# Three kinds of small TensorE work moved into the middle of the attention slots, and PSUM units given by hand

## The chip, the cores and the metric

The kernel runs on one core of one Trainium2 chip. The metric is the device time of one execution in microseconds. Before the change it is 1381.16 us, the median of 3 runs (1380.94 to 1382.31). The core has five engines, each with its own instruction stream in program order: TensorE (PE, matrix products, with weight loads shown apart as PEld), VectorE (DVE), ScalarE (ACT), GpSimd (POOL) and SyncE (SP, which only starts transfers here). They meet at semaphores.

## The reference

Two transformer blocks on 256 tokens of 1024 channels, in fp32. The change touches the first block. It makes one wide projection `h @ w_in` and feeds three branches:

```
(c_glu, c_gate, d_q, d_k, d_v, d_gate, x_q, x_gate, merge) = jnp.split(
    h @ w_in[l], IN_SPLITS, axis=-1)
y_conv = conformer_conv_branch(c_glu, c_gate, ...)   # 31-tap causal convolution per channel, layer norm
y_diff = differential_attention_branch(d_q, d_k, d_v, d_gate, ...)   # 8 heads, two softmaxes each
y_mem  = memory_cross_attention_branch(x_q, x_gate, mem_h, w_mem_kv, ...)  # 4 heads over 256 memory rows
y = g[:, :, 0] * y_conv + g[:, :, 1] * y_diff + g[:, :, 2] * y_mem
x = x + y @ w_out[l]
```

In the differential branch q and k are normed per head (a sum of squares over 64 channels), each head has `a = p[:, :, 0] - lam * p[:, :, 1]` with `p` a causal softmax, and the output `a @ v` is normed over 128 channels. The memory branch norms q and k over 256 channels and has plain softmaxes. The second block (stick-breaking attention, an RG-LRU, and a lookup of 16 experts for each of 8 heads) follows.

## The kernel before, in words

All projections are cut into **slots** of 512 output columns. A slot is two **pieces** of 256 columns. For a piece the queue of SP loads 1 MB of weights into `w_raw`; ACT rounds them into `w_hi` (L667, `hi(p)`), DVE writes the rest into `w_lo` (L1117, `lo(p)`); and PE makes 48 matrix products of 256 columns (L368: high by high, high by low, low by high). `w_hi` and `w_lo` have three buffers, so `hi(p)` waits until PE has finished piece p-3, and the two engines split the pieces of slot n+1 while PE works on slot n. On ACT and DVE the function `ahead(s)` does this, one piece after the other, and can run a list of functions `between` the two. `project(s)` on PE has such a list too; in the attention slots before the change it is empty.

The order of every engine is written out by hand. The list `attention` has 18 slots: n = 0 to 5 are q0, k0, v0, q1, k1, v1, 6 and 7 are xq0 and xq1, 8 and 9 xk0 and xk1, 10 and 11 xv0 and xv1, 12 to 17 the merge gates m0 to m5. Around each slot stand the steps of the attention, skewed against each other so that each finds its input ready:

- `head_sums`: ones times squares (L401, L407), for the q or k of the slot before. Its square comes from ACT (L737), and after it come a Ln and an Exp on ACT (L744, L749) and a scaling on DVE (L1221). `diff_norm_sums` (L417) is the same for the attended heads, half dn0 (heads 0 to 3) and dn1; its square is L788 on ACT, which stands there behind the exponentials (L768) of the head of that slot. ACT does the squares of dn0 at the end of n = 10, and PE sums them at n = 11.
- `diff_scores(h)` at n = h+3 (L429), then on DVE the softmax of that head (L1243 to L1268) with the exponentials on ACT (L768) in its middle; `diff_turn(h)` at n = h+4 transposes the probabilities (L439), ACT copies them from PSUM (L776), and `diff_values(h)` at n = h+5 multiplies with v (L448, L449). `cross_scores`, `cross_turn`, `cross_values` (L459, L470, L481) do the same for the memory heads at n = h+11, h+12 and h+13.
- `turn_input("mem")` transposes the normed memory (L389) into the second input pair, ahead of slot v0 (n = 2). Slots xk0 and later use it.
- Between its pieces DVE also does three taps of the convolution each (L1132). POOL does five of the eight channel tiles of the convolution alone (L1762, L1766). `conv_mean` on PE (L492), after the slots dg0 and dg1 which follow the attention slots, waits for all eight tiles.

PSUM is three **units** of two banks and two single banks, each a ring: `take` gives the next one in turn, and a user waits until the prior holder's readers have marked it free. Slots, sums and scores all take units in the order in which they stand on PE.

## Time and profile before

| what | value |
|---|---|
| device time, median of 3 | 1381.16 us |
| the profiled execution, own time | 1380.68 us |
| its span in the trace | 1378.9 us |
| PE busy, share of span | 84% |
| DVE, ACT, POOL busy | 70%, 41%, 41% |
| mean granted PE clock | 0.975 of full |

The span begins at 0 and all times below count from there. The 18 attention slots run from about 72 to 349 us, slots dg0 and dg1 to 371.8 us, the rest of the first block to about 529 us. From about 700 us on the expert lookup runs, with the transfer engines busy 96% of the time. A timeline row gives start, length, engine, line, operation, names and shape, and in brackets the idle time of the engine ahead of it with what ended it. Matrix products overlap, so 96 of them that start 0.12 us apart show 0.28 us each; an fp32 product is two records, one of the rounded type is one.

### The profile page before, as it was taken

What the parts mean: (1) busy time and instruction counts of PE and PEld (TensorE: products, weight loads), DVE (VectorE), ACT (ScalarE), POOL (GpSimd) and SP (SyncE); (2) the same over time, 40 slices, a digit from 0 to 9 for tenths busy, and PEclk for the clock granted to TensorE, in tenths of its full rate; (3) what the DMA queues carried; (4) which work ended last, traced back from release to release, by engine and by line L of the source; (5) the groups of instructions that cost most, each with busy time, mean ns of one, the idle gap of its engine ahead of it and who ended that gap; (6) DMA issues with size and microseconds to landing.
All of it is one profiled execution on the core that took longest, in us unless ns stands there. A gap on an engine that the chain in (4) does not pass through costs nothing.

```text
span 1378.9 us, 16624 instructions
## 1 busy us (share of the span) xinstructions
PE 1163.5 (84%) x6104; PEld 819.6 (59%) x6104; DVE 972.0 (70%) x1937; ACT 569.0 (41%) x1022; POOL 561.9 (41%) x576
## 2 busy tenths in 40 slices
PE   5999898999999998976898877777877777777787
PEld 5999788899999998975895322222322222222222
DVE  4488888894567655656577777777777777777554
ACT  5376656664345334885342322222222222222221
POOL 0099999999600000000023434444444444444431
PEclk9999999999999999998999999999999999999999
DMA  6644343354536644420458999999999999999995
GB/s 222 198 139 143 102 123 123 122 163 153 174 123 218 210 153 152 147 92 31 153 181 335 424 426 424 424 425 423 425 424 425 424 424 419 422 413 404 425 425 226
DMA packets 137331, 374.43 MB, mean 272 GB/s; under 512 B 6816, under 2 KB 103072, under 8 KB 104352
## 3 DMA queue, kind: packets, MB, share of 16 engines
q0 software_dynamic: 36864, 268.45, 46.8%
q1 hardware_dynamic: 98048, 99.62, 22.3%
q10 hardware_dynamic: 2336, 5.29, 1.1%
q8 instruction: 48, 0.79, 0.2%
q14 instruction: 35, 0.29, 0.1%
HBM read 372.29 MB, written 1.05 MB: 271 GB/s over the span
## 4 chain that ended last, share of the span: by engine, by line
PE 38%; DMA 34%; DVE 16%; ACT 6%; issue 5%; ACTq 0%; POOL 0%; POOLq 0%; DVEq 0%
PE unit L368 29%; DMA big<-in_experts,big 16%; DMA row<-in_experts,big 7%; DMA w_raw<-in_experts,big 6%; PE unit L585 6%; DMA conv_in<-in_experts,big 5%; DVE w_lo L1117 3%; DVE conv_acc L1132 3%; DVE work L1464 2%; ACT probs L899 1%; ACT probs L768 1%; DVE big L1221 1%; DVE probs L1264 1%; DMA w_raw<-in_w_in 1%; DVE probs L1268 1%
## 5 line engine op out<-in xcount | busy, mean ns | idle before, releaser
L368 PE MATMUL unit<-in_hi,w_hi 128*128 128x256 f32 x1216 | 351.8, 289 | 8.7 <-DVE probs L1336 4.8
L368 PE MATMUL unit<-in_lo,w_hi 128*128 128x256 f32 x1216 | 347.3, 286 | 0.0
L368 PE MATMUL unit<-in_hi,w_lo 128*128 128x256 f32 x1216 | 347.2, 286 | 0.0
L1117 DVE TENSOR_TENSOR w_lo<-w_raw,w_hi 128x2048 fp32r<-128x2048 f32 x94 | 219.0, 2332 | 122.7 <-ACT w_hi L667 122.7
L899 ACT ACTIVATE probs<-ident,big 128x128 f32<-128x128 f32 x256 | 102.8, 401 | 462.9 <-DVE big L1476 462.9
L585 PE MATMUL unit<-big,probs 128*128 128x512 f32 x452 | 224.0, 621 | 63.9 <-ACT probs L899 63.8
L368 PEld LDWEIGHTS unit<-in_hi,w_hi 128*128 128x128 f32 x1216 | 237.2, 195 | 11.2 <-issue 5.9
L368 PEld LDWEIGHTS unit<-in_lo,w_hi 128*128 128x128 f32 x1216 | 237.0, 195 | 0.9 <-issue 0.7
L1774 POOL DMA_INDIRECT row<-in_experts,big x58 | 63.5, 1095 | 426.9 <-DVE big L1457 343.4
L368 PEld LDWEIGHTS unit<-in_hi,w_lo 128*128 128x128 f32 x1216 | 236.7, 195 | 0.0
L667 ACT CAST w_hi<-w_raw 128x2048 fp32r<-128x2048 f32 x94 | 177.0, 1899 | 128.9 <-PE unit L368 84.7
L585 PEld LDWEIGHTS unit<-big,probs 128*128 128x128 f32 x452 | 79.5, 191 | 204.8 <-ACT probs L899 144.4
L1774 POOL DMA_INDIRECT big<-in_experts,big x113 | 120.0, 1062 | 168.2 <-PE unit L585 151.9
L1464 DVE CUSTOM_DVE_ANT_0 work<-big 128x1024 f32<-128x1024 f32 x113 | 138.0, 1222 | 65.7 <-DMA big<-in_experts,big 65.7
L585 PE MATMUL unit<-row,probs 128*128 128x512 f32 x232 | 116.9, 634 | 33.0 <-ACT probs L899 32.8
L1766 POOL TENSOR_TENSOR conv_acc<-conv_acc,big 128x256 f32<-128x256 f32 x150 | 139.5, 930 | 12.5
L1762 POOL TENSOR_SCALAR big<-conv_in,vec 128x256 f32<-128x256 f32 x150 | 141.5, 944 | 2.9
L585 PE MATMUL unit<-w_raw,probs 128*128 128x512 f32 x224 | 109.6, 619 | 27.4 <-ACT probs L899 27.3
L585 PEld LDWEIGHTS unit<-row,probs 128*128 128x128 f32 x232 | 41.5, 195 | 106.0 <-ACT probs L899 74.2
L585 PEld LDWEIGHTS unit<-w_raw,probs 128*128 128x128 f32 x224 | 39.4, 191 | 95.2 <-ACT probs L899 65.7
L1464 DVE CUSTOM_DVE_ANT_0 work<-big,row 128x1024 f32<-128x1024 f32 x58 | 70.7, 1221 | 31.2 <-DMA row<-in_experts,big 31.2
L1774 POOL DMA_INDIRECT w_raw<-in_experts,big x56 | 60.1, 1073 | 77.2 <-PE unit L585 68.7
(246 smaller groups left out, 1699.0 us busy)
## 6 DMA issues: line engine op xcount, KB each, us to landing
w_raw<-in_w_in SPq DMA_DIRECT2D x58, 1024.0 KB, 5.2
w_raw<-in_w_mem_kv SPq DMA_DIRECT2D x8, 1024.0 KB, 5.3
w_raw<-in_w_out SPq DMA_DIRECT2D x8, 1024.0 KB, 5.2
w_raw<-in_w_query SPq DMA_DIRECT2D x8, 1024.0 KB, 5.4
w_raw<-in_w_diff_proj SPq DMA_DIRECT2D x4, 1024.0 KB, 5.6
w_raw<-in_w_x_proj SPq DMA_DIRECT2D x4, 1024.0 KB, 5.1
w_raw<-in_w_conv_proj SPq DMA_DIRECT2D x4, 1024.0 KB, 5.2
big<-in_x ACTq DMA_DIRECT2D x2, 1024.0 KB, 7.5
```

What stands on the lines that cost most here:

```text
L368: m = e.matmul(unit[:, to:to + 256], fixed, moving, start=start, stop=stop)
L585: m = e.matmul(unit[:, half * 512:(half + 1) * 512], diag_places[g % 12], UV.ap(g)[:, D + half * 512:D + (half + 1) * 512], start=n == 0, ...
L667: e.copy(w_split[p % 3][0][:, :, :], w_raw[p % 2][:, :, :]).then_inc(*mark("hi", p))
L768: a = e.activation(p[:, m, c], p[:, m, c], ACT.Exp, bias=few[:, i + m:i + m + 1], accum_out=few[:, 4 + i + m:5 + i + m])
L899: e.activation(diag_places[g % 12], ident[:, :], ACT.Copy, scale=here).then_inc(*mark("diag", g))
L1117: e.tensor_tensor(lo_part[:, :, :], w_raw[p % 2][:, :, :], hi_part[:, :, :].bitcast(F32), ALU.subtract).then_inc(*mark("lo", p))
L1132: i = e.scalar_tensor_tensor(out=dst, in0=src, scalar=tap, in1=dst, op0=ALU.mult, op1=ALU.add)
L1221: i = e.scalar_tensor_tensor(out=part, in0=part, scalar=gain[:, j:j + 1], in1=work.ap(name)[:, 0:n].rearrange("p (g t) -> p g t", t=T), op ...
L1464: e.tensor_tensor_reduce(out=work.ap(("dot", g))[:, 0:D], in0=h3[:, t, :], in1=UV.ap(g)[:, 0:D], scale=1.0, scalar=0.0, op0=ALU.mult, op1= ...
L1762: e.tensor_scalar(product, src, tap, 1.0, ALU.mult, ALU.mult).then_inc(*mark("pool_product", (t, k)))
L1766: e.tensor_tensor(dst, dst, product, ALU.add).then_inc(*mark("pool_tap", None, *done))
L1774: e.indirect_dma_start(out=UV.ap(g), out_offset=None, in_=experts, in_offset=bass.IndirectOffsetOnAxis(ap=expert[t][:, n:n + 1], axis=0)). ...
```

## The change

On PE the sums of squares, the transposes of the probabilities and the turn of the memory are no longer done around a slot; they are handed to `project` as a list that runs between its two pieces. ACT (Ln, Exp, copy of the transposed probabilities, rounding of the memory) and DVE (scaling, the rest of the memory) move along into the middle of their `ahead`. The transposes of head h move from behind slot h+4 to the middle of slot h+5 (cross heads: from behind h+12 to the middle of h+13), the turn of the memory from ahead of slot 2 to the middle of slot 3, and the sums from behind slot n to its middle. `take` accepts a unit number: slots alternate between units 0 and 1, sums take the one of the two that the running slot does not have, scores always take unit 2. The values of head 7 stand in the common place, behind slot 12.

```
     def take(self, use, place=None):
-        i = self.n % len(self.buffers)
-        self.n += 1
+        i = self.n % len(self.buffers) if place is None else place
+        self.n = i + 1
...
 # PE
             for n, s in enumerate(attention):
-                if s.name == "v0":
-                    turn_input("mem", mem_tm,
-                               lambda half: (("scaled", "mem", half, 0), ("scaled", "mem", half, 1)))
-                project(s)
-                if s.name == "m0":
-                    diff_values(DIFF_HEADS - 1)
+                midway, other = [], 1 - n % 2
                 if pending in HEAD_NORMS:
-                    head_sums(pending)
+                    midway.append(partial(head_sums, pending, other))
                 elif pending:
-                    diff_norm_sums(int(pending[2:]))
+                    midway.append(partial(diff_norm_sums, int(pending[2:]), other))
+                if s.name == "q1":
+                    midway.append(partial(turn_input, "mem", mem_tm, lambda half: (
+                        ("scaled", "mem", half, 0), ("scaled", "mem", half, 1)), (other, 2)))
+                if 0 <= n - 5 < DIFF_HEADS:
+                    midway.append(partial(diff_turn, n - 5))
+                if 0 <= n - 13 < X_HEADS:
+                    midway.append(partial(cross_turn, n - 13))
+                project(s, midway, n % 2)
                 pending = s.name if s.name in HEAD_NORMS else {10: "dn0", 12: "dn1"}.get(n)
-                if 0 <= n - 5 < DIFF_HEADS - 1:
+                if 0 <= n - 5 < DIFF_HEADS:
                     diff_values(n - 5)
-                if 0 <= n - 4 < DIFF_HEADS:
-                    diff_turn(n - 4)
...
-            project(slot["dg0"])
+            project(slot["dg0"], place=0)
...
 # ACT
-                if name == "v0":
-                    turn_input("mem", "mem_norm_g")
-                ahead(s)
+                midway = []
+                if pending in HEAD_NORMS:
+                    midway.append(partial(head_root, pending))
+                elif pending:
+                    midway.append(partial(inverse_root, pending, 4 * T, P))
+                if name == "q1":
+                    midway.append(partial(turn_input, "mem", "mem_norm_g"))
+                if 0 <= n - 5 < DIFF_HEADS:
+                    midway.append(partial(diff_turned, n - 5))
+                if 0 <= n - 13 < X_HEADS:
+                    midway.append(partial(cross_turned, n - 13))
+                ahead(s, between=midway)
...
 # DVE
-                ahead(s)
+                midway = []
+                if pending in HEAD_NORMS:
+                    midway.append(partial(head_scale, pending))
+                elif pending:
+                    midway.append(partial(diff_norm_scale, pending))
+                if s.name == "q1":
+                    midway.append(partial(turn_input, "mem", "mem_norm_g"))
+                ahead(s, between=midway)
```

PE at the end of slot 11 (xv1) before. L417 is the sum of squares of dn0 (its squares lie in `work0`), L448 and L449 the values of head 6, L439 the transposes of head 7, L459 the scores of memory head 0:

```order
L368 MATMUL unit2<-w1_hi,in1_hi 128x256
L368 MATMUL unit2<-w1_hi,in1_lo 128x256
L368 MATMUL unit2<-w1_lo,in1_hi 128x256
L417 MATMUL unit0<-work0,ones 128x512 x2
L448 MATMUL bank1<-probs_t0,big2 128x256
L449 MATMUL bank1<-probs_t0,big2 128x128
L439 MATMUL bank0<-ident,probs1 128x128 x3
L459 MATMUL unit1<-big5,big4 128x256 x4
L368 MATMUL unit2<-in0_hi,w2_hi 128x256
```

PE in the middle of slot 11 now, between its piece in `w0` and its piece in `w1` (lines are one higher in the changed file). L418 is the sum of squares of dn0, L440 the transposes of head 6:

```order
L369 MATMUL unit1<-w0_hi,in1_hi 128x256
L369 MATMUL unit1<-w0_hi,in1_lo 128x256
L369 MATMUL unit1<-w0_lo,in1_hi 128x256
L418 MATMUL unit0<-work0,ones 128x512 x2
L440 MATMUL bank0<-ident,probs0 128x128 x3
L369 MATMUL unit1<-w1_hi,in1_hi 128x256
```

The sum of dn0 has moved ahead of the second piece of the same slot, 48 products earlier than before; head 7's transposes are no longer there and stand in the middle of slot 12.

ACT at the same place before, from the exponentials of head 7 (L768) over the squares of dn0 (L788) to the Ln and Exp of dn0 (L744, L749) and the copy of head 7's transposed probabilities (L776):

```order
L768 ACTIVATE probs1,col<-probs1,col 128x256 x2
L768 ACTIVATE probs1,col<-probs1,col 128x128 x2
L788 ACTIVATE work0<-big0 128x1024
L667 CAST w2_hi<-w_raw0 128x2048
L667 CAST w0_hi<-w_raw1 128x2048
L759 COPY big6<-unit2 128x2x512
L744 ACT_TABLE_LOAD
L744 ACTIVATE work0<-unit0,col 128x1024
L749 ACT_TABLE_LOAD
L749 ACTIVATE work0<-work0 128x1024
L782 COPY big0<-bank1 128x256
L776 COPY probs_t1<-bank0 128x384
```

And now, the same span of ACT:

```order
L768 ACTIVATE probs1,col<-probs1,col 128x256 x2
L768 ACTIVATE probs1,col<-probs1,col 128x128 x2
L788 ACTIVATE work0<-big0 128x1024
L667 CAST w2_hi<-w_raw0 128x2048
L744 ACT_TABLE_LOAD
L744 ACTIVATE work0<-unit0,col 128x1024
L749 ACT_TABLE_LOAD
L749 ACTIVATE work0<-work0 128x1024
L776 COPY probs_t0<-bank0 128x384
L667 CAST w0_hi<-w_raw1 128x2048
L759 COPY big6<-unit1 128x2x512
L782 COPY big0<-bank1 128x256
```

Ln, Exp and the copy of the probabilities have moved between the two castings; the squares of dn0 keep their place behind the exponentials of head 7.

## Rows read from the trace of the kernel before

**Rows 1.** Windows: length, busy PE, PEld, DVE, ACT, POOL, then clock, DMA share, GB/s.

```profile
200.00:250.00 50.00, 42.99 (x316) 40.46 (x315) 44.69 (x55) 33.77 (x50) 47.75 (x54) 0.97 0.35 110
300.00:350.00 50.00, 50.00 (x395) 49.06 (x394) 28.98 (x24) 22.19 (x22) 45.84 (x49) 1.00 0.48 153
```

**Rows 2.** Waits from 150 to 263 us: total, times, longest.

```profile
DVE col L1257 <- ACT probs L768: 11.6, 6, 1.9
PE bank L439 <- DVE probs L1268: 9.5, 5, 4.0
PE unit L368 <- DVE w_lo L1117: 4.0, 5, 0.8
PE unit L417 <- ACT work L788: 2.1, 1, 2.1
```

**Rows 3.** Timeline of DVE, one slot's round.

```profile
222.65 2.28 DVE L1117 TENSOR_TENSOR w_lo<-w_raw,w_hi 128x2048 fp32r<-128x2048 f32 x1
...
231.45 2.11 DVE L1221 SCALAR_TENSOR_TENSOR big<-big,vec,work 128x512 f32<-128x512 f32 x2
...
237.84 0.18 DVE L1257 RECIPROCAL col<-col 128x4 f32<-128x4 f32 x1 [1.93 <-ACT probs L768]
...
241.12 2.28 DVE L1117 TENSOR_TENSOR w_lo<-w_raw,w_hi 128x2048 fp32r<-128x2048 f32 x1
```

**Rows 4.** Timeline of ACT, the readers of slots dg0 and dg1.

```profile
360.49 1.02 ACT L818 ACTIVATE work<-unit 128x1024 f32<-128x1024 f32 x1 [3.80 <-PE unit L368]
...
372.01 1.02 ACT L818 ACTIVATE work<-unit 128x1024 f32<-128x1024 f32 x1 [3.80 <-PE unit L368]
```

**Rows 5.** The page's group of the castings on ACT: busy and mean ns of one.

```profile
L667 ACT CAST w_hi<-w_raw 128x2048 fp32r<-128x2048 f32 x94 | 177.0, 1899 | 128.9 <-PE unit L368 84.7
```

**Rows 6.** Timeline of ACT, slots 10 and 11.

```profile
242.33 1.28 ACT L744 ACT_TABLE_LOAD   x1
243.62 0.69 ACT L744 ACTIVATE work<-unit,col 128x512 f32<-128x512 f32 x1
...
256.20 1.04 ACT L788 ACTIVATE work<-big 128x1024 f32<-128x1024 f32 x1
```

**Rows 7.** Timeline of PE, from slot 11 to the start of slot 12.

```profile
243.45 0.39 PE L368 MATMUL unit<-w_hi,in_hi 128*128 128x256 f32 x1 [0.79 <-DVE w_lo L1117]
...
257.29 3.09 PE L417 MATMUL unit<-work,ones 128*128 128x512 f32 x4 [2.06 <-ACT work L788]
260.17 1.06 PE L448 MATMUL bank<-probs_t,big 128*128 128x256 f32 x2
...
261.78 1.89 PE L459 MATMUL unit<-big 128*128 128x256 f32 x8
263.32 0.47 PE L368 MATMUL unit<-in_hi,w_hi 128*128 128x256 f32 x1
```

**Rows 8.** Timeline of DVE, its idle times ahead of the first softmax.

```profile
97.54 1.37 DVE L1221 SCALAR_TENSOR_TENSOR big<-big,col,work 128x1024 f32<-128x1024 f32 x1 [0.76 <-ACT work L749]
...
112.90 1.33 DVE L1221 SCALAR_TENSOR_TENSOR big<-big,vec,work 128x1024 f32<-128x1024 f32 x1 [1.62 <-ACT work L749]
```

**Rows 9.** Windows of PE: length, busy, granted clock, DMA share, GB/s.

```profile
169.20:172.70 3.50, 3.46 (x16) 0.51 0.06 8
258.00:261.40 3.40, 3.40 (x7) 0.50 0.02 5
529.20:534.50 5.30, 5.30 (x25) 0.50 0.01 3
```

**Rows 10.** Timeline of POOL, its last products.

```profile
351.94 2.51 POOL L1762 TENSOR_SCALAR big<-conv_in,vec 128x256 f32<-128x256 f32 x1
...
355.37 0.48 POOL L1762 TENSOR_SCALAR big<-conv_in,vec 128x256 f32<-128x256 f32 x1
...
368.02 0.74 POOL L1766 TENSOR_TENSOR conv_acc<-conv_acc,big 128x256 f32<-128x256 f32 x1
```

**Rows 11.** Timeline of PE, conv_mean.

```profile
371.81 3.61 PE L492 MATMUL unit<-conv_acc,ones 128*128 128x256 f32 x16
```

More of the change, by code:

```diff
@@ L1 @@
 from contextlib import ExitStack
+from functools import partial
 import concourse.bass as bass
@@ L91, in __init__, with take @@
         self.place, self.prior, self.holder, self.n = {}, {}, [None] * len(buffers), 0
-    def take(self, use):
-        i = self.n % len(self.buffers)
-        self.n += 1
+    def take(self, use, place=None):
+        i = self.n % len(self.buffers) if place is None else place
+        self.n = i + 1
         self.place[use], self.prior[use], self.holder[i] = i, self.holder[i], use
@@ L342, in pe, with project @@
             W = Reached(at)
-            def project(s, between=()):
-                unit = units.take(s.name)
+            def project(s, between=(), place=None):
+                unit = units.take(s.name, place)
                 in_hi, in_lo = pairs.ap(s.pair)
@@ L376, in project, with turn_input @@
                             f()
-            def turn_input(pair, src, scaled):
+            def turn_input(pair, src, scaled, places=(None, None)):
                 for half in range(2):
                     name = f"{pair} turn{half}"
-                    unit = units.take(name)
+                    unit = units.take(name, places[half])
                     for bank in range(2):
@@ L391, in turn_input, with head_sums @@
                         m.then_inc(*mark("turned", (pair, 2 * half + bank)))
-            def head_sums(name):
-                sq, unit = work.ap(name), units.take(name + " sums")
+            def head_sums(name, place=None):
+                sq, unit = work.ap(name), units.take(name + " sums", place)
                 for wait in W(("sq", name), units.free(name + " sums"), ("const", None)):
@@ L409, in head_sums, with diff_norm_sums @@
                 m.then_inc(*mark("sums", name))
-            def diff_norm_sums(i):
+            def diff_norm_sums(i, place):
                 name = f"dn{i}"
-                sq, unit = work.ap(name), units.take(name + " sums")
+                sq, unit = work.ap(name), units.take(name + " sums", place)
                 for wait in W(("sq", name), units.free(name + " sums")):
@@ L421, in diff_scores @@
             def diff_scores(h):
-                unit = units.take(f"d{h}")
+                unit = units.take(f"d{h}", 2)
                 for wait in W(("normed", f"q{h // 4}"), ("normed", f"k{h // 4}"),
@@ L452, in cross_scores @@
             def cross_scores(h):
-                unit = units.take(f"x{h}")
+                unit = units.take(f"x{h}", 2)
                 for wait in W(("normed", f"xq{h // 2}"), ("normed", f"xk{h // 2}"),
@@ L613, in pe @@
                     cross_values(n - 13)
-                if 0 <= n - 12 < X_HEADS:
-                    cross_turn(n - 12)
                 if 0 <= n - 11 < X_HEADS:
                     cross_scores(n - 11)
-            project(slot["dg0"])
+            project(slot["dg0"], place=0)
             project(slot["dg1"])
@@ L951, in act @@
                         *mark("merge", i, ("unit free", name)))
-                if pending in HEAD_NORMS:
-                    head_root(pending)
-                elif pending:
-                    inverse_root(pending, 4 * T, P)
                 pending = name if name in HEAD_NORMS else {10: "dn0", 12: "dn1"}.get(n)
@@ L958, in act @@
                     diff_attended(n - 5)
-                if 0 <= n - 4 < DIFF_HEADS:
-                    diff_turned(n - 4)
                 if 0 <= n - 3 < DIFF_HEADS:
@@ L966, in act @@
                     cross_attended(n - 13)
-                if 0 <= n - 12 < X_HEADS:
-                    cross_turned(n - 12)
                 if 0 <= n - 11 < X_HEADS:
@@ L1535, in dve @@
             for n, s in enumerate(attention):
-                if s.name == "v0":
-                    turn_input("mem", "mem_norm_g")
-                ahead(s)
+                midway = []
[6 more added lines that the diff above has]
+                ahead(s, between=midway)
                 if n == 0:
@@ L1541, in dve @@
                     scale_tokens("mem", mem_tm, mem_tm)
-                if pending in HEAD_NORMS:
-                    head_scale(pending)
-                elif pending:
-                    diff_norm_scale(pending)
                 pending = s.name if s.name in HEAD_NORMS else {10: "dn0", 12: "dn1"}.get(n)
```

## The prediction

> **What bounds the kernel now.** I read the busy shares by windows first, then the waits of the attention slots, then one slot as a timeline. The windows show two regimes. From 200 to 250 us PE is busy 43 of 50 us and DVE 44.7; from 300 to 350 us PE is busy all 50 and DVE 29 [rows 1]. So PE waits for something only in the slots with a differential softmax. The waits say for what: 9.5 us ahead of the transposes L439 until DVE has the probabilities, 4.0 us ahead of the next slot, 2.1 us ahead of the sum of squares dn0 (L417) until ACT has the squares [rows 2]. The first two make 13.5 us, which a better order on PE seems to be able to take back.
>
> The timeline of DVE says that it can't. Its round from one first `w_lo` to the next is 241.12 - 222.65 = 18.5 us, and all its idle time in it is the 1.93 us that it waits for the exponentials of its own softmax [rows 3]; that pair is also its whole wait in the list, 11.6 us in 6 times [rows 2]. It does not wait for PE there. PE's own work in such a slot is 11.5 us for the 96 products (the readers of two bare slots start at 360.49 and 372.01, 11.52 apart [rows 4]) and some 4 us for the small steps. Up to the end of the softmax of head 7 the pace is DVE's, whatever order PE has; after that it is PE's own.
>
> **The change part by part.**
>
> *Transposes and scores.* No instruction is added or removed on PE, DVE or ACT; all terms are about places. The transposes of head h go half a slot or more behind the end of its softmax, so the wait of L439 goes. What is late next is the values: they need the copy that ACT makes of the transposes, and it stands now behind the exponentials of the next head, a casting, and Ln and Exp. With the exponentials done at 237.8 [rows 3], a casting of 1.9 [rows 5], two table loads with two functions of twice 1.29 + 0.7 = 4.0 [rows 6] and about 0.5 for the copy, the values could start at 244.2, and with some 1.5 us of values and scores (both estimates) slot 11 starts about 245.7, where it starts now at 243.45 [rows 7]. So PE still stands still some 3 us in each slot, in another place. All of it lies beside DVE, whose next softmax needs those scores at 241.12 + (231.45 - 222.65) + 2.1 = 252.0 [rows 3], 6 us later. Gain 0, cost 0.
>
> *Scaling on DVE.* It stands now one `w_lo` and three taps after the softmax, (231.45 - 222.65)/2 = 4.4 us behind 241.12, at 245.5 [rows 3], and needs Ln and Exp, which are done at 237.8 + 1.9 + 4.0 = 243.7 for the 512 wide ones and about 0.9 later for the 1024 wide ones. That holds with 0.9 us to spare at least. Cost 0. If the cover went, each microsecond would count in each of the six slots, since DVE sets the pace.
>
> Here a rule speaks against the change. The trace shows a load of 1.28 us and the Ln 1.29 us behind the load's start [rows 6]. The Trainium skill (ScalarE: Activation LUTs, What ACT_TABLE_LOAD costs) says that a switch of sets costs a drain beside its load, about 2.66 us in all. By that rule two switches would take 2.7 us more than my sum, the scaling would wait up to 1.9 us per slot, and the time would be some 8 us longer still. By the row nothing happens, and I go by the row.
>
> *Start.* Ahead of the first softmax DVE waits 0.76 and 1.62 us for Ln and Exp [rows 8]. Sums that are taken half a slot earlier can shorten this. The bounds are 0 and 2.4 us; as the scaling also moves forward, it keeps part of the wait. I take 1.0 us gained; call it G.
>
> *The sum of squares dn0.* This is the term that decides. Its squares (L788) stand on ACT behind the exponentials of head 7, which are the end of DVE's part in the softmax of slot 10. They are ready at 256.20 + 1.04 = 257.24 [rows 6], or 257.24 - G, by DVE's pace. Now PE has finished all of slot 11 by then and waits 2.06 us. After the change it has done only the first piece, waits (from about 251 until 256, by the slot start above), and has the second piece still to do: 11.52/2 = 5.76 us [rows 4] that used to lie under DVE's pace come behind it. From there on PE waits for nothing [rows 1] and all of it counts. Cost 5.76 - G = 4.8 us.
>
> *The clock.* PE's granted clock is 0.50, the lower level, 1.2 GHz, in 258.0 to 261.4, behind the wait of 2.06 us, and in another place it stays at 0.50 for 5.3 us [rows 9]. In the first, half of 3.4 us is lost, 1.7 us; the sum took 3.09 there [rows 7]. After the change PE idles some 5 us ahead of dn0 and would start at about 256.2. If the clock comes back at 261.4 as now, 5.2 us run at half, 2.6 lost, 0.9 more than before. Bounds: 0 more, and 2.65 (half of the 5.3 us of the other place on top). I take 0.9.
>
> *Turn of the memory, units, cross heads.* The turn is the same 16 + 8 + 8 instructions one slot later, needed first in slot xk0; the cross heads' transposes sit in PE's own stream with the same length; with fixed units a slot waits for the copy of the slot two before. None has a wait in PE's stretch after 263 now [rows 1], each has half a slot of room. Bounds -0.5 and +1; I take 0.
>
> *conv_mean.* POOL's last product ends at 368.76 [rows 10], and conv_mean starts at 371.81 right behind dg1 [rows 11]. A later PE only widens that. Everything behind it hangs on it, and shifts as a whole.
>
> Sum: 4.8 + 0.9 = 5.7 us later, so 1380.7 + 5.7 = 1386.4 us against the profiled execution; that one was 0.5 below the median of the runs, so I say 1386.6.
>
> **The rivals.**
>
> *A. Not slower: the waits go and POOL becomes the bound.* If DVE's pace were not binding and PE took back its 13.5 us, it would reach conv_mean at 358 and wait for POOL until 368.8. But DVE runs ahead with PE: the `w_lo` of the next slot then falls under POOL's last products, and a POOL product beside a `w_lo` takes 2.51 where it takes 0.48 otherwise [rows 10], 2 us. That ends POOL at about 370.8, a gain of 1.0, or of 3.0 at best without this. PE would have idled 10 us and would start conv_mean at the low clock, 1.7 to 2.65 lost: 1380.7 - 3.0 + 1.7 to 1380.7 - 1.0 + 2.65, so 1379.4 to 1382.4. It decides from the point at which PE reaches conv_mean before 368.8. Against it: DVE's round has no idle time that PE could give back.
>
> *B. The early gain is larger and pays for dn0.* G at its upper bound 2.4 and no further loss of clock: 5.76 - 2.4 = 3.4, so 1384.1, 1384.3 against the median. G above 3 would end inside no change. For it: both idle times of rows 8 wait for just the operations that move.
>
> *C. The scaling on DVE waits in every slot.* It starts once Ln and Exp are 0.9 us later than assumed; up to 1 us beyond that in six slots is 1 to 6 us on top: 1388 to 1393. For it: the margin is thin, and a contention with other work could use it up. Against: the row of the load, which shows nothing beside the load itself [rows 6]. The drain of the Trainium skill's page (ScalarE: Activation LUTs, What ACT_TABLE_LOAD costs) would be this case.
>
> *D. Faster by clearly more than the bound*, if the sum dn0 finds its squares ready. ACT would have to do them 6 us earlier than DVE lets it. I see nothing for it.
>
> **How the numbers follow.** Forecast (shift 4.0 to 7.5 with the clock's bounds) 0.66; B 0.10; A 0.10; C 0.10; D and unknown gains 0.04. What a measurement of this kernel can tell from no change is 0.2%, 2.8 us: faster is under 1378.4, slower over 1384.0. Faster takes D and a little of A, 0.05; the same takes the rest of A and a third of B, 0.12; slower the other cases, 0.83. The range 1382.4 to 1389.4 holds the forecast with its bounds, B, the top of A and the bottom of C.
>
> **What would show it.** Right: the transposes have no wait; the values (L449 in the changed file) wait some 3 us per slot for ACT's copy; DVE's round stays at 18.5 us; L418 of dn0 waits 4 to 7 us for ACT's squares at about 256 us and the clock behind it is 0.5; conv_mean starts at about 377.5, with no wait, and each later stage is later by the same amount. Wrong: a shorter round of DVE, a wait of conv_mean for POOL (A), idle time ahead of L1222 in slots 4 to 9 (C), or a sum dn0 without a wait (D).

## The result, and the profile after

The changed kernel takes 1388.53 us (median of 13 runs, 1384.30 to 1389.59) against 1381.16 us (13 runs, 1379.34 to 1382.31): 7.4 us slower by the medians. The ratio is 1.0048 with a 95% interval of 1.0039 to 1.0057; that is the ratio of the means, 1387.75 and 1381.08 us, 6.7 us apart. The 13 times of the changed kernel lie in two groups, five from 1384.30 to 1386.99 us and eight from 1388.46 to 1389.59, and the median is in the longer one. The profiled execution, 1385.57 us, is of the shorter group, 4.9 us over the profiled one of before.

| | before | after |
|---|---|---|
| profiled execution, own time | 1380.68 | 1385.57 us |
| span | 1378.9 | 1383.8 us |
| mean granted PE clock, profiled execution | 0.975 | 0.970 |
| PE busy, share of span | 84% | 84% |
| DVE, ACT, POOL busy | 70%, 41%, 41% | 70%, 41%, 40% |

The waits of PE and DVE from 150 to 263 us in the kernel after (total, times, longest), against [rows 2]:

```profile
DVE col L1258 <- ACT probs L768: 11.6, 6, 1.9
PE bank L449 <- ACT probs_t L776: 9.7, 4, 3.3
PE unit L418 <- ACT work L788: 5.6, 1, 5.6
PE unit L369 <- DVE w_lo L1118: 1.7, 1, 1.7
```

The transposes (L440) don't wait any more; the values (L449) do, 9.7 us where the transposes had 9.5. DVE's own wait is the same 11.6 us. And dn0 waits 5.6 us for its squares instead of 2.1.

The timeline of PE after, from the end of slot 10 to slot 12, and conv_mean, against [rows 7, 11]:

```profile
240.99 0.70 PE L449 MATMUL bank<-probs_t,big 128*128 128x256 f32 x2 [0.22 <-ACT probs_t L776]
...
242.70 0.39 PE L369 MATMUL unit<-w_hi,in_hi 128*128 128x256 f32 x1
...
254.28 3.78 PE L418 MATMUL unit<-work,ones 128*128 128x512 f32 x4 [5.56 <-ACT work L788]
257.85 0.85 PE L440 MATMUL bank<-ident,probs 128*128 128x128 f32 x3
258.35 0.56 PE L369 MATMUL unit<-w_hi,in_hi 128*128 128x256 f32 x1
...
266.82 0.47 PE L369 MATMUL unit<-in_hi,w_hi 128*128 128x256 f32 x1
...
375.62 3.61 PE L493 MATMUL unit<-conv_acc,ones 128*128 128x256 f32 x16
```

Slot 11 starts at 242.70 (243.45 before), its sum dn0 at 254.28 (257.29 before), but slot 12 at 266.82 (263.32 before): the second piece of slot 11 now stands behind the sum. conv_mean starts at 375.62 without an idle time (371.81 before).

The timeline of DVE after, two rounds:

```profile
216.37 0.18 DVE L1258 RECIPROCAL col<-col 128x4 f32<-128x4 f32 x1 [1.93 <-ACT probs L768]
...
234.87 0.18 DVE L1258 RECIPROCAL col<-col 128x4 f32<-128x4 f32 x1 [1.93 <-ACT probs L768]
...
253.31 0.18 DVE L1258 RECIPROCAL col<-col 128x4 f32<-128x4 f32 x1 [1.93 <-ACT probs L768]
```

The rounds are 18.50 and 18.44 us, those before 18.48 and 18.48. Before, the reciprocal of head 6 stood at 237.84 [rows 3] and that of head 7 here:

```profile
256.32 0.18 DVE L1257 RECIPROCAL col<-col 128x4 f32<-128x4 f32 x1 [1.93 <-ACT probs L768]
```

**A fixed point to count from.** The start of the span moves between executions. DVE's second write of `conv_in`, right ahead of the attention slots, is the same step in every kernel, at 68.62 us before and at 67.79 after, and at 67.40 to 68.82 over the 14 profiles. The timeline of DVE, before and then after:

```profile
68.62 1.22 DVE L1528 SCALAR_TENSOR_TENSOR conv_in<-work,unit 128x1024 f32<-128x1024 f32 x1 [2.54 <-ACT work L921]
```

```profile
67.79 1.22 DVE L1529 SCALAR_TENSOR_TENSOR conv_in<-work,unit 128x1024 f32<-128x1024 f32 x1 [2.54 <-ACT work L921]
```

The first three columns count from it: the reciprocal of head 7 on DVE, the start of slot 12 on PE, and conv_mean. "Round" is the mean of the seven rounds between the eight reciprocals, the last two columns are the time from conv_mean to the turn of the second block's input, and from there to the end of the span. All in us, from one profile each.

| kernel | head 7 | slot 12 | conv_mean | round | to turn | to end |
|---|---|---|---|---|---|---|
| before | 187.70 | 194.70 | 303.19 | 18.21 | 157.35 | 849.7 |
| after | 185.52 | 199.03 | 307.83 | 18.11 | 155.85 | 852.3 |
| after_again | 185.54 | 198.15 | 306.95 | 18.11 | 157.35 | 849.3 |
| after_again2 | 185.61 | 198.96 | 307.75 | 18.12 | 157.35 | 850.8 |
| before_dn0_mid | 187.09 | 199.97 | 308.47 | 18.26 | 157.35 | 850.2 |
| before_heads_mid | 185.51 | 191.39 | 302.99 | 18.05 | 159.10 | 849.8 |
| before_turns_mid | 187.14 | 193.07 | 302.72 | 18.27 | 157.61 | 852.5 |
| after_dn0_next | 185.47 | 191.10 | 303.69 | 18.07 | 159.03 | 850.0 |
| after_squares | 185.53 | 196.48 | 305.28 | 18.11 | 158.98 | 851.8 |
| heads_mid_pool4 | 186.38 | 192.24 | 302.23 | 18.22 | 158.96 | 853.0 |
| after_squares_pool4 | 185.45 | 196.92 | 306.31 | 18.14 | 159.03 | 849.8 |
| after_squares_pool4_taps | 175.92 | 186.77 | 298.08 | 16.83 | 159.14 | 849.1 |
| turns_first | 185.58 | 191.19 | 302.45 | 18.12 | 155.83 | 852.4 |
| tile_shared | 164.77 | 172.42 | 287.84 | 15.41 | 157.43 | 851.6 |

Read along the second row: head 7 comes 2.2 us earlier, slot 12 is 4.3 us later, conv_mean 4.6 us. Up to the turn 1.5 us are got back, by the clock (last section), and behind it 2.6 are lost, at least in part by the clock; with the 0.8 us by which the fixed point comes earlier that makes 4.9.

The row "before" is itself one profile. before_dn0_mid, whose order up to slot 10 is the old one, has head 7 at 187.09, 0.6 us earlier than the profile of before. So the early gain is 1.6 to 2.2 us.

### The profile page after: what moved, and what is told of

Read it like the earlier page. It is cut to its first block, busy times and chain, and to the rows that moved or that the text cites. A ratio compares the mean times of both kernels' runs of the same rounds, so it can differ in the third digit from the quotient of the medians.

```text
span 1383.8 us, 16623 instructions
## 1 busy us (share of the span) xinstructions
PE 1164.6 (84%) x6104; PEld 819.8 (59%) x6104; DVE 972.1 (70%) x1937; ACT 569.1 (41%) x1022; POOL 555.8 (40%) x576
## 4 chain that ended last, share of the span: by engine, by line
PE 38%; DMA 34%; DVE 18%; ACT 6%; issue 5%; ACTq 0%; POOL 0%; POOLq 0%; DVEq 0%
PE unit L369 27%; DMA big<-in_experts,big 16%; DMA row<-in_experts,big 7%; PE unit L586 6%; DMA w_raw<-in_experts,big 6%; DMA conv_in<-in_experts,big 5%; DVE w_lo L1118 4%; DVE conv_acc L1133 3%; DVE work L1465 2%; ACT probs L768 1%; ACT probs L899 1%; DVE probs L1265 1%; DMA w_raw<-in_w_in 1%; DVE big L1222 1%; DVE probs L1269 1%
## 5 line engine op out<-in xcount | busy, mean ns | idle before, releaser
L1768 POOL TENSOR_TENSOR conv_acc<-conv_acc,big 128x256 f32<-128x256 f32 x150 | 143.2, 954 | 12.5
L1764 POOL TENSOR_SCALAR big<-conv_in,vec 128x256 f32<-128x256 f32 x150 | 133.3, 889 | 2.9
```

The source lines that it names most:

```text
L1764: e.tensor_scalar(product, src, tap, 1.0, ALU.mult, ALU.mult).then_inc(*mark("pool_product", (t, k)))
L1768: e.tensor_tensor(dst, dst, product, ALU.add).then_inc(*mark("pool_tap", None, *done))
```

## Experiments

Times are medians; ratios are to the kernel before, run on the same chip, with the 95% interval.

**after_dn0_next: dn0 in the middle of slot 12.** On PE, ACT and DVE alike:

```
-                pending = s.name if s.name in HEAD_NORMS else {10: "dn0", 12: "dn1"}.get(n)
+                pending = s.name if s.name in HEAD_NORMS else {11: "dn0", 12: "dn1"}.get(n)
```

> The changed kernel with one difference: the sum of squares dn0, with its Ln, Exp and scaling, stands in the middle of slot 12 and no longer of slot 11 (dn1 stays in slot 13). Theory 'place of dn0': in the trace of the changed kernel slot 12 starts at 266.82 us because dn0 waits for its squares until 254.28 with half of slot 11 still to do. Without it slot 11 ends at about 254, and slot 12 waits for its w_lo, which is written at 258.8, so it starts at about 259; dn0 then costs 1.9 us as a sum without a wait, and conv_mean starts at 375.6 - 7.8 + 1.9 = 369.7 us instead of 375.62. The time is 5 to 6 us under the changed kernel and about 2 us under the kernel before: 1378 to 1381 us. Theory 'clock': the changed kernel loses its time to twice as much low clock in the slots (three stretches of 6.8 us against three of 3.4 us), which waits in every slot bring about; then the place of dn0 gives back 1 to 2 us only, 1386 to 1388 us.

Measured: 1383.23 us, ratio 1.0016 (1.0007 to 1.0025), 5.3 us under the changed kernel by the medians (4.4 by the ratios, 0.0032 of 1381). Against the kernel before it is slower, not 2 us faster as expected. Slot 12 starts at 258.50 us, as worked out. PE's timeline:

```profile
258.50 0.39 PE L369 MATMUL unit<-in_hi,w_hi 128*128 128x256 f32 x1
...
264.35 1.88 PE L418 MATMUL unit<-work,ones 128*128 128x512 f32 x4
...
274.20 0.70 PE L449 MATMUL bank<-probs_t,big 128*128 128x256 f32 x2 [1.89 <-ACT probs_t L776]
```

The place of dn0 is the larger part of the loss, and the theory of the clock, which expected 1386 to 1388 us, falls. But of 7.9 us at slot 12 only 4.1 are left at conv_mean: the sum costs 1.9 there, and the values of head 7 wait 1.89 us for a copy that now stands behind Ln and Exp of dn0, a wait that I had not counted. Against the kernel before it is 0.5 us late at conv_mean, and 1.7 more go behind it (last section).

**before_dn0_mid: the one part alone, in the kernel before.** Its three places follow the same pattern:

```
-                project(s)
+                mid = pending == "dn0"
+                project(s, [step] if mid else ())     # step: the sum of the name in pending
...
+                if step and not mid:
+                    step()
```

> The kernel before, in which the sum of squares dn0 alone (with Ln, Exp and scaling) moves into the middle of slot 11. Theory 'place of dn0': the half slot of 5.76 us that lay ahead of the wait comes behind it, nothing is gained earlier, and the low clock takes up to 2 us more: conv_mean at 377.5 to 379.5 us, 1387 to 1389 us. Theory 'clock' (the loss comes from waits in all slots): dn0 alone costs 0 to 2 us, 1381 to 1383 us.

Measured: 1386.66 us, ratio 1.0049 (1.0036 to 1.0062). PE's timeline:

```profile
256.02 3.78 PE L418 MATMUL unit<-work,ones 128*128 128x512 f32 x4 [6.30 <-ACT work L790]
...
267.94 0.47 PE L369 MATMUL unit<-in_hi,w_hi 128*128 128x256 f32 x1
```

This one move gives the ratio of the whole change, with a wait of 6.30 us. From head 7 to slot 12 it is 267.94 - 255.06 = 12.9 us instead of 263.32 - 256.32 = 7.0, 5.9 more (255.06 is the reciprocal of head 7 in this run). conv_mean is 5.3 us later by the table. The expectation was 377.5 to 379.5 us for conv_mean and 1387 to 1389 for the time; they are 376.44 and 1386.66, just under both. Its six times lie in two groups too: four from 1385.60 to 1387.15 us and two at 1390.15 and 1390.59.

**before_heads_mid: only the sums of q, k, xq, xk.** As above with `mid = pending in HEAD_NORMS`.

> The kernel before, in which only the sums of squares of q, k, xq and xk (with Ln, Exp and scaling) move into the middle of the next slot; dn0, dn1, the transposes and the memory's turn stay. Theory 'early gain': all of the 3.0 us by which the exponentials of head 7 came earlier in the changed kernel (253.31 against 256.32 us) come from these sums. The sum dn0 starts at about 254.3, conv_mean at 368.8 to 369.3 us (the last product on POOL ends at 368.8), and the time is 2.5 to 3 us under the kernel before: about 1378.5 us. Rival: the gain comes from the transposes, whose wait went; then this kernel stays at 1381 us.

Measured: 1381.63 us, ratio 1.0003 (0.9995 to 1.0012). The time was expected 2.5 to 3 us lower and is unchanged. In the table head 7 comes 2.2 us earlier (1.6 against before_dn0_mid), exactly as in the changed kernel: these sums are all of the early gain. Slot 12 is 3.3 us earlier. But PE and POOL at conv_mean show where it ends:

```profile
370.70 5.38 PE L493 MATMUL unit<-conv_acc,ones 128*128 128x256 f32 x16 [2.95 <-issue]
```

```profile
369.31 0.48 POOL L1766 TENSOR_SCALAR big<-conv_in,vec 128x256 f32<-128x256 f32 x1
369.88 0.72 POOL L1770 TENSOR_TENSOR conv_acc<-conv_acc,big 128x256 f32<-128x256 f32 x1
```

conv_mean starts 0.1 us behind POOL's last product and has 2.95 us idle ahead of it, and behind that the clock is low (5.38 us for 3.61). The early gain came as expected, but POOL's end does not stay at 368.8: its last product ends at 370.6 us, and counted from the fixed point it is 2.8 us later (302.89 against 300.14).

**before_turns_mid: only the transposes.**

```
-                project(s)
+                project(s, [lambda: diff_turn(n - 5) if 0 <= n - 5 < DIFF_HEADS else None,
+                            lambda: cross_turn(n - 13) if 0 <= n - 13 < X_HEADS else None])
...
-                if 0 <= n - 4 < DIFF_HEADS:
-                    diff_turn(n - 4)
```

> The kernel before, in which only the transposes of the probabilities (differential and memory heads, with the copies on ACT) move half a slot back. Theory of the prediction: PE's wait moves from the transposes to the values, DVE's round stays at 18.5 us, and the time is 1381 us within 1 us. Rival: the transposes are what gave the 3.0 us, or a part above the 2.3 us of the start (0.7 us): 1378 to 1380.5 us. Rival 'clock': the waits that are then shorter and more frequent cost low clock, 1383 to 1385 us.

Measured: 1380.69 us, ratio 0.9998 (0.9989 to 1.0006). PE's waits from 150 to 263 us:

```profile
PE unit L368 <- DVE w_lo L1111: 7.6, 5, 1.8
PE bank L448 <- ACT probs_t L773: 4.9, 4, 3.0
```

13.5 us of waits were [rows 2], 12.5 are these: they moved and DVE's round stayed, 18.27. In the time there is no gain and no cost. On the way slot 12 is 1.6 us earlier than in the profile of before, with 0.6 of it there at head 7 already, as in before_dn0_mid, and no low stretch behind dn0; POOL then ends at 370.29 us, 0.1 us ahead of conv_mean.

**after_squares: ACT's squares ahead of the exponentials of head 7.**

```
+                if n == 10:
+                    diff_norm_squares(0)
                 if 0 <= n - 3 < DIFF_HEADS:
                     diff_exps(n - 3)
-                if n == 10:
-                    diff_norm_squares(0)
```

> The changed kernel with two steps of ACT exchanged at the end of slot 10: the squares of dn0 stand ahead of the exponentials of head 7 and no longer behind them. ACT is idle for 7.49 us there in the trace of the changed kernel, and the squares need only heads 0 to 3. Theory 'the wait of dn0 is one for ACT's order': the squares are ready at about 245 us, L418 has no wait, and the next thing that is late is the values of head 6, whose copy stands behind Ln and Exp of dn0: exponentials done at 253.2, casting 1.9, Ln and Exp with their loads 4.7, copy 0.46, so 260.3; with 2.2 us of values and scores slot 12 starts at 262.5 us instead of 266.82, conv_mean at 371.3 instead of 375.62, and the time is 4 to 5 us under the changed kernel: 1381.5 to 1384 us. Theory 'the cost is the pace of DVE and the clock, not this wait': 1387 to 1389 us.

Measured: 1383.37 us, ratio 1.0022 (1.0012 to 1.0031), 5.2 us under the changed kernel by the medians, 3.6 by the ratios. PE's timeline:

```profile
249.25 1.88 PE L418 MATMUL unit<-work,ones 128*128 128x512 f32 x4
...
261.02 1.07 PE L449 MATMUL bank<-probs_t,big 128*128 128x256 f32 x2 [3.81 <-ACT probs_t L776]
...
264.99 0.47 PE L369 MATMUL unit<-in_hi,w_hi 128*128 128x256 f32 x1
```

Its sum dn0 has no wait. As expected the values are what is late next; they come 0.7 us later than worked out, and the clock is low behind their wait (1.07 us for 0.59), so that slot 12 and conv_mean gain 2.6 us by the table, not 4.3. The time lies in the expected range, but this path gives only half of the 5.2 us; the rest of the difference of the medians it does not explain.

**heads_mid_pool4 and after_squares_pool4: POOL with four tiles.**

```
-POOL_TILES = (3, 4, 5, 6, 7)
+POOL_TILES = (4, 5, 6, 7)
...
-                ahead(s, between=midway)
+                ahead(s, between=midway, convolve=3 if n < 11 else 4)
```

In heads_mid_pool4, which is the kernel before with the sums of the heads moved, the list is `[step] if mid else ()` in place of `midway`.

> The kernel before with the sums of squares of q, k, xq and xk in the middle (as in before_heads_mid), and with one of the five convolution tiles of POOL given to DVE (POOL does tiles 4 to 7; DVE four taps per gap instead of three from slot 11 on). In before_heads_mid slot 12 started at 259.10 us, 4.2 us earlier than in the kernel before, but conv_mean started at 370.70, with 2.95 us idle ahead, right behind POOL's last product at 370.60. Theory 'POOL ends the gain': without that tile conv_mean starts at 259.1 + 108.5 = 367.6 us with no idle time ahead, and the time is 3 us lower than before_heads_mid: 1378 to 1379 us. Rival 'the early slots' gain is given back elsewhere' (DVE with 31 more taps, or the clock): 1381 to 1383 us.

> As after_squares, with POOL doing tiles 4 to 7 alone (DVE four taps per gap from slot 11 on). Theory 'POOL is not the bound here': POOL's last product ended at 364.2 us in the changed kernel and PE came to conv_mean at 375.6, and with the squares first at 371.3, so a shorter POOL gives nothing: the same time as after_squares within 1 us, unless POOL's products beside DVE's work slow DVE, where a shorter round of DVE would give 1 to 3 us.

Measured: heads_mid_pool4 1380.83 us, ratio 0.9999 (0.9989 to 1.0009); after_squares_pool4 1384.60 us, 1.0031 (1.0020 to 1.0041). The second is 1.2 us over after_squares where at most 1 us was expected, with overlapping intervals: relieving POOL gives nothing there. The profile of the first is its longest of 12 executions (1384.81 us; they go from 1378.15), so its stages are weak evidence. In it the idle time ahead of conv_mean is gone, but conv_mean comes only 0.8 us earlier than in before_heads_mid, not 3: from slot 12 it takes 110.0 us and not 108.5, with waits for DVE that has the tile now (the transposes of a memory head wait 0.76 us for its softmax). It does not decide between POOL and "given back elsewhere"; both are there.

**after_squares_pool4_taps: fewer taps where DVE sets the pace.**

```
-                ahead(s, between=midway, convolve=3 if n < 11 else 4)
+                ahead(s, between=midway, convolve=3 if n < 3 else 2 if n < 11 else 4)
...
-            convolve_some(len(taps))
...
-                ahead(slot[f"dg{i}"])
+                ahead(slot[f"dg{i}"], convolve=4)
+                if i == 1:
+                    convolve_some(len(taps))
```

> As after_squares_pool4, with the taps of the convolution on DVE moved out of the slots that DVE paces: two per gap instead of three in slots 3 to 10, four in slots 11 to 17 and in dg0 and dg1. Theory 'DVE's round paces slots 3 to 10': each round has two taps fewer, 1.4 us at 2.10 us for three, so the round falls from 18.5 to 17.1 us, the exponentials of head 7 end 8 x 1.4 = 11 us earlier, at about 242 us, conv_mean starts at about 360 us, and the time is 10 us under after_squares_pool4: 1370 to 1374 us. Rival 'PE's wait for ACT's copy sets the round as well': the round stays over 18 us and less than 4 us is gained, 1378 to 1382 us.

Measured: 1378.30 us, ratio 0.9979 (0.9970 to 0.9988). The round falls by 1.3 us, as expected, and head 7 comes 9.5 us earlier. The time, expected at 1370 to 1374 us, misses that by 4.3: slot 12 is 10.2 us earlier, conv_mean 8.2, with 0.99 us of waiting for the last taps on DVE (PE's timeline):

```profile
366.84 3.72 PE L493 MATMUL unit<-conv_acc,ones 128*128 128x256 f32 x16 [0.99 <-DVE conv_acc L1133]
```

**turns_first: transposes and their copy ahead of the sums in the middle.** On after_squares, PE and ACT alike:

```
+                if 0 <= n - 5 < DIFF_HEADS:
+                    midway.append(partial(diff_turn, n - 5))
                 if pending in HEAD_NORMS:
                     midway.append(partial(head_sums, pending, other))
...
-                if 0 <= n - 5 < DIFF_HEADS:
-                    midway.append(partial(diff_turn, n - 5))
```

> As after_squares, with the order in the middle of a slot exchanged on PE and ACT: first the transposes of the probabilities and their copy, then the sums of squares with Ln and Exp. The copy that the values wait for (15.8 us in six waits of L449 in after_squares) then comes up to 4.7 us earlier. Theory 'these waits lie beside DVE in slots 3 to 10, and only the last, of 3.81 us in slot 11, counts': the waits nearly go, the exponentials of two heads stay 18.1 us apart, slot 12 starts 3 to 3.8 us earlier than the 264.99 us of after_squares, and the time is 3 to 4 us lower: 1379.5 to 1380.5 us. Rival 'PE's waits in all slots set the pace too': 15 us of waits go and the round shrinks below 17 us, under 1375 us. Rival 'the clock': fewer waits, less low clock, another 2 us lower.

Measured: 1380.88 us, ratio 1.0000 (0.9991 to 1.0009). PE's waits from 150 to 263 us:

```profile
PE unit L369 <- DVE w_lo L1118: 7.5, 8, 1.7
PE bank L449 <- ACT probs_t L776: 7.3, 5, 2.5
```

8.5 us of waits for the copy went and 7.1 us of waits for `w_lo` came, with the same round of 18.12 us. That shows that in slots 3 to 10 PE's waits cost nothing; only the last one did, and slot 12 is 5.3 us earlier. Of these 5.3 us, 2.8 are left at conv_mean: in between PE waits 1.6 us where after_squares waits for nothing, nearly all of it at the first values of a memory head (PE's timeline), and the other 0.9 us are not traced:

```profile
290.36 2.00 PE L482 MATMUL bank<-probs_t,big 128*128 128x256 f32 x8 [1.43 <-ACT probs_t L805]
```

POOL is close behind. Its last product is stretched from 0.74 to 2.65 us beside a `w_lo` of DVE (timeline of DVE, then of POOL, then of PE):

```profile
367.63 2.46 DVE L1118 TENSOR_TENSOR w_lo<-w_raw,w_hi 128x2048 fp32r<-128x2048 f32 x1 [1.43 <-ACT w_hi L667]
```

```profile
367.47 0.48 POOL L1764 TENSOR_SCALAR big<-conv_in,vec 128x256 f32<-128x256 f32 x1
368.03 2.65 POOL L1768 TENSOR_TENSOR conv_acc<-conv_acc,big 128x256 f32<-128x256 f32 x1
```

```profile
371.20 3.61 PE L493 MATMUL unit<-conv_acc,ones 128*128 128x256 f32 x16
```

PE comes 0.5 us behind it without an idle time, so POOL is all but the bound. The time of 1380.88 us is 0.4 over the expected range.

**tile_shared: the convolution divided by the pace of each stage.** On turns_first:

```
-                ahead(s, between=midway)
+                ahead(s, between=midway, convolve=3 if n < 3 else 1 if n < 11 else 4)
...
-            convolve(POOL_TILES[4:])
+            convolve((3,), 14)      # of tile 3 the taps from 14 on; DVE has those below
```

`POOL_TILES` is (4, 5, 6, 7) here too, and the dg slots take four taps as in after_squares_pool4_taps.

> As turns_first, and the convolution is divided anew: of tile 3 DVE does the taps 0 to 13 and POOL the rest after its tiles 4 to 7; DVE does three taps per gap in slots 0 to 2, one in slots 3 to 10, four from slot 11 to dg1. Theory 'DVE paces slots 3 to 10': four taps fewer per slot than in the changed kernel, 2.8 us at 2.10 us for three, so the round falls from 18.1 to 15.3 us, the exponentials of head 7 end at about 234 us, slot 12 starts at about 243 us, conv_mean at about 353 us, POOL ends at 307 + 17 x 1.85 = 338 us, and the time is 1362 to 1366 us. Rival 'PE becomes the pace' (11.5 us of products, some 3 us of small steps and the waits between them): the round stays at 16 us or more, 1367 to 1373 us.

Measured: 1367.09 us (4 runs, 1366.36 to 1367.96), ratio 0.9905 (0.9890 to 0.9920): 13 us faster than the kernel before, and than the changed one by more. It is above the 1362 to 1366 us of the theory and in the range of its rival, 1367 to 1373, but the round decides between the two. The timeline of DVE, and the window of 200 to 250 us of [rows 1]:

```profile
217.20 0.18 DVE L1259 RECIPROCAL col<-col 128x4 f32<-128x4 f32 x1 [1.93 <-ACT probs L768]
...
232.69 0.18 DVE L1259 RECIPROCAL col<-col 128x4 f32<-128x4 f32 x1 [1.93 <-ACT probs L768]
```

```profile
200.00:250.00 50.00, 50.00 (x385) 47.73 (x384) 43.06 (x51) 36.06 (x56) 47.83 (x53) 1.00 0.44 139
```

The round is 15.41 us on the mean (15.3 expected, 16 or more by the rival); PE is busy 50 of 50 us at full clock, where it was 43. With that PE is at its limit as well. Slot 12 starts at 240.34 us, 2.7 earlier than worked out, but conv_mean comes at 355.76 and not at 353: the first values of a memory head wait 3.66 us for their copy (PE's timeline):

```profile
272.49 2.88 PE L482 MATMUL bank<-probs_t,big 128*128 128x256 f32 x8 [3.66 <-ACT probs_t L805]
```

**after_again, after_again2: two more profiles of the changed kernel.**

> The changed kernel once more, for a second profile. Its executions fall in two groups, 1384.3 to 1387.0 and 1388.5 to 1389.6 us, and the profiled one (1385.57) is of the first. Theory 'the groups differ in the clock alone': a profile of the second group shows more or longer stretches of low clock in the PE-bound stages (each of 3.4 us costs 1.7) and the same waits; one of the first group shows the same stretches as before. Rival: one more wait, or a POOL or DMA that is later.

> The same kernel a third time, with the same expectations as after_again.

Measured: 1384.11 and 1385.30 us, both of the shorter group, so they don't show what the longer group has. They show how far one kernel's profiles differ: slot 12 by 0.9 us, the way from conv_mean to the turn by 1.5, the way to the end by 3.0.

## Why the prediction was right, point by point

- **Pace of DVE, transposes and values: right.** No wait at the transposes, 9.7 us at the values, the longest 3.3 ("some 3 us"); DVE's round stays. before_turns_mid shows the price of that part in the time, none, and turns_first and the two kernels with fewer taps in slots 3 to 10 show the cause: PE's waits in slots 3 to 10 change their place and nothing follows, and the round shrinks by more than 0.1 us only when DVE gets less to do there.
- **Scaling on DVE: right, nothing.** L1222 has no idle time in slots 4 to 9. The load ahead of Exp took 1.28 us at 259.23 and Exp started 1.29 behind it, at 260.52, as in [rows 6]. The drain that the Trainium skill (ScalarE: Activation LUTs, What ACT_TABLE_LOAD costs) puts beside each switch does not show in this trace; by that rule rival C would have come.
- **Early gain G: too small, and only in part from where I put it.** I took 1.0 in bounds of 0 to 2.4; it is 2.2 against the profile of before, 1.6 against before_dn0_mid, and all from the sums of q, k, xq and xk (before_heads_mid). My step named only the waits ahead of the first softmax and took DVE's round as fixed. At the first reciprocal 1.5 us of the 2.2 are there; the other 0.7 comes in the rounds (18.11 against 18.21 us, seven times). DVE's idle time in them is the same, 13.1 us, but the ten scalings take 11.4 us there and not 12.2. Why they are shorter in their new place no run shows.
- **dn0: right.** Half a slot, 5.76, less G of 2.2 makes 3.6, and with the clock 4.3 at slot 12. The one part alone gives the ratio of the whole change (1.0049, interval 1.0036 to 1.0062) although it lacks the early gain: conv_mean is 5.3 us later there, and 4.6 in the whole change.
- **Clock behind dn0: right in size.** 4.3 - 3.6 = 0.7 against 0.9. The sum takes 3.78 us where it took 3.09, and the window of 252.5 to 259.3 us is at the lower level:

```profile
252.50:259.30 6.80, 5.02 (x11) 0.50 0.00 0
```

- **Turn, units, cross heads, conv_mean.** From slot 12 to conv_mean 108.8 us against 108.5. conv_mean at 375.62 instead of the 377.5 predicted: 1.2 us of it are G, 0.8 the earlier fixed point, and the clock (0.2 less) and the way from slot 12 (0.3 more) all but cancel. No run has the turn of the memory or the fixed units by themselves; that they cost nothing is read from these 108.8 us and from the early gain alone.
- **What I had not counted:** the stages behind, and the clock in them. They add 1.1 us in the profiled executions. In the medians the loss is 2.5 us larger than there, so that the forecast of 5.4 over the median is under the measured 7.4 although the mechanism gave only 4.6. So two sizes were off, in opposite directions: G, and what is lost behind conv_mean and in the longer executions, which I had put at nothing. That 1386.6 comes within 2 us of the median is partly luck. There is also a slip in the sum: with the 0.5 us between the profiled execution and the median, 1386.4 makes 1386.9.

Rival A (POOL becomes the bound) didn't come, since PE was late; but its mechanism is there in before_heads_mid, where PE stands still 2.95 us until POOL ends, and all but there in before_turns_mid and turns_first, where PE comes 0.1 and 0.5 us behind it. I had worked out POOL's end at 370.8 and 1379.4 to 1382.4 us. Counted from the fixed point and put on the time scale of the profile of before (68.62 added), it ends at 371.5, 371.2 and 370.6 us in these three, at 368.8 before and at 365.0 in the changed kernel, and the three times are 1380.7 to 1381.6. POOL is later where PE is early, as the rival said. Its price is not settled: with POOL relieved, heads_mid_pool4 gained 0.8 us at conv_mean and 0.8 in the median, and waits for DVE account for part of the rest. Against the profile of before, Rival B's G of 2.4 was nearer than my 1.0.

Rival D was dismissed with a wrong reason. I wrote that ACT "would have to do them 6 us earlier than DVE lets it". DVE doesn't hold the squares; they only stood behind the exponentials in ACT's order, and ACT was idle 7.5 us ahead of those (timeline of ACT, before):

```profile
254.43 0.51 ACT L768 ACTIVATE probs<-probs,col 128x256 f32<-128x256 f32 x1 [7.53 <-DVE col L1254]
```

after_squares does them earlier with two lines exchanged, and the wait goes. It is still slower than the kernel before (1.0022), since the values of head 6 are late next; the rival's "faster by clearly more" does not follow from the ready squares alone.

## What to carry to other kernels

A step that waits for another engine is cheapest behind the work of its own engine that can be done first; moved half a slot ahead, that half slot is paid. Before waits of one engine are taken away, ask whose round they lie in: here 13 us of PE's waits were worth nothing, and two taps less for DVE per slot brought the last softmax 9.5 us forward. And a gain ends at the next engine that joins (POOL here), which can itself become slower by it.

## What the runs showed of the hardware

**The same wait is not always followed by a low clock.** conv_variance waits 2.06 us for ACT in the kernel before and in after_dn0_next; the sum takes 3.72 us there and 5.41 here (timelines of PE, before and then after_dn0_next, and the window behind the wait in the latter: length, busy, granted clock, DMA share, GB/s):

```profile
388.99 3.72 PE L503 MATMUL unit<-work,ones 128*128 128x256 f32 x16 [2.06 <-ACT work L984]
```

```profile
388.27 5.41 PE L504 MATMUL unit<-work,ones 128*128 128x256 f32 x16 [2.06 <-ACT work L985]
```

```profile
388.60:392.00 3.40, 3.40 (x10) 0.50 0.16 55
```

In 6 of the 14 profiles a low stretch follows this wait, which is 2.06 us in each. Near 500 us it is the other way round: a stretch in the kernel before, none in the changed one. Both have one around the turn (from 527.7 and 529.0 us), and behind it, near 550 us, only the changed kernel has another (windows of PE, before and then after):

```profile
500.40:503.80 3.40, 3.40 (x18) 0.50 0.00 0
...
547.20:551.00 3.80, 3.80 (x34) 1.00 0.86 278
```

```profile
500.40:507.00 6.60, 3.54 (x29) 1.00 0.42 145
549.60:553.00 3.40, 3.40 (x18) 0.51 0.86 272
```

The column "to turn" of the table takes three values, 155.8, 157.4 to 157.6 and 159.0 to 159.1 us, by no, one or two such stretches in between, beside the one at the turn that all have: 1.5 to 1.7 us for one of 3.4 us at the half clock, on an engine that is the bound there. Two profiles of one kernel (after, after_again) differ in it as well, so a difference of 1 to 3 us between two single profiles need not be the edit's. Behind the turn it is alike: from it to the turn of `h3`, the last input that PE turns, the 14 profiles take 146.6 to 146.7, 148.1 to 148.2 or 149.5 to 149.8 us (146.6 before, 149.8 after), and the five of the last group have a low stretch just behind the turn, between 545 and 552 us, and no other has. The step from 146.6 to 148.1 us is not traced.

**The spread of the changed kernel goes with its clock.** Over its 13 runs time and mean granted clock have a correlation of -0.86, 0.76 us for each 0.001; its mean clock is 0.9685, that of 29 runs of the kernel before 0.972. By that slope the difference would be worth 2.7 us, about what the medians differ beyond the profiles. But that is argued: within the 29 runs of the kernel before the slope is 0.18 us for each 0.001, with a correlation of -0.32. What the runs do show is where the longer group comes: in the changed kernel and in before_dn0_mid, the two with dn0's long wait in slot 11 (its two long runs have a clock of 0.965, the four others 0.971), and not in after_dn0_next, whose 11 runs end at 1385.06 us. One run of such a length is elsewhere, 1389.79 us in after_squares_pool4. In which stage the longer runs lose it stays open, as no profile fell among them.

**POOL's products are stretched beside DVE's `w_lo`:** the last one to 2.65 us from 0.74 in turns_first. In the changed kernel, where PE is late and DVE with it, POOL ended at 364.2 us, 4.6 us earlier than before (3.7 from the fixed point).
